# First norm of each layer by token tile: turns, router and shared expert of tile 0 while tile 1 is normalised, and the output product by column halves

## The reference, cut to what matters

```python
for l in range(2):
    h = merged @ w_out[l]                       # 256 x 1024 times 1024 x 1024
    x = layer_norm(DN_ALPHA * x + h, ln1_g[l], ln1_b[l])
    idx, wts = route(x, router_w[l], router_bias[l])       # 1024 -> 64 scores per token, top 8 of 64
    u = x @ shared_w_gate_up[l]                            # 1024 -> 512
    shared = (silu(u[:, :256]) * u[:, 256:]) @ shared_w_down[l]
    y = shared + routed_experts(x, idx, wts, expert_w_gate_up[l], expert_w_down[l])
    x = layer_norm(DN_ALPHA * x + y, ln2_g[l], ln2_b[l])
```

## Time and profile before

| | |
|---|---|
| median of 3 runs | 1595.6 us (1593.86 to 1598.8) |
| profiled execution, its own time | 1594.94 us |
| its span, first to last instruction | 1593.1 us |
| PE busy | 1535.1 us, 96% of the span |
| DVE, ACT busy | 567.2 us, 413.2 us |
| mean granted TensorE clock | 0.983 |
| transfers | 495.85 MB, 311 GB/s over the span |

### The profile page before, as it was taken

How to read it: one execution, slowest core, us unless ns; L and a number is a source line. 1 busy time by engine, 2 the same in 40 slices (tenths; PEclk the granted TensorE clock), 3 DMA queues, 4 the chain that set the end, 5 groups by cost and what they waited for, 6 DMA issues and landing times.

```text
span 1593.1 us, 21647 instructions
## 1 busy us (share of the span) xinstructions
PE 1535.1 (96%) x8770; PEld 954.1 (60%) x8770; DVE 567.2 (36%) x1011; ACT 413.2 (26%) x653; POOL 34.5 (2%) x30
## 2 busy tenths in 40 slices
PE   7999998999999999999789999989999999999996
PEld 7899985554454444445388999865444544544442
DVE  4567735222222222222445677352222222222224
ACT  4545422121111112112235544221211211111111
POOL 0101000000000000000001110000000000000000
PEclk9999998999999999999989999989999999999998
DMA  8544458699999999699733544577999999996991
GB/s 290 174 170 142 155 210 355 250 425 423 418 418 415 405 415 414 248 414 417 279 104 109 186 159 159 213 315 280 428 423 416 420 408 410 417 412 247 415 416 77
DMA packets 79740, 495.85 MB, mean 311 GB/s; under 512 B 6080, under 2 KB 11456, under 8 KB 46656
## 3 DMA queue, kind: packets, MB, share of 16 engines
q1 hardware_dynamic: 77392, 491.31, 76.4%
q10 hardware_dynamic: 2288, 3.67, 0.7%
HBM read 493.92 MB, written 1.05 MB: 311 GB/s over the span
## 4 chain that ended last, share of the span: by engine, by line
PE 93%; DVE 2%; DMA 2%; ACT 1%; issue 1%; SPq 0%; DVEq 0%
PE bank L1384 27%; PE bank L1227 19%; PE bank L1410 14%; PE bank L1339 8%; PE bank L1356 8%; PE bank L1297 4%; PE bank L1184 3%; PE bank L1314 2%; DMA ring_w<-in_w_in 2%; PE bank L1396 1%; PE bank L1371 1%; PE bank L1305 1%; PE bank L1347 1%; ACT w_hi L590 1%; PE bank L1239 1%; PE bank L1265 1%
## 5 line engine op out<-in xcount | busy, mean ns | idle before, releaser
L1227 PE MATMUL bank<-x_hi,w_hi 128*128 128x256 f32 x688 | 198.4, 288 | 3.5 <-ACT arena L639 1.9
L1227 PE MATMUL bank<-x_hi,w_lo 128*128 128x256 f32 x688 | 195.3, 284 | 0.0
L1227 PE MATMUL bank<-x_lo,w_hi 128*128 128x256 f32 x688 | 195.3, 284 | 0.0
L1121 DVE SCALAR_TENSOR_TENSOR hid<-hid,gate_s,bank 128x256 f32<-128x256 f32 x64 | 30.8, 481 | 401.2 <-ACT hid L701 401.2
L1384 PE MATMUL bank<-gu_a,arena 128*64 128x512 f32 x768 | 170.1, 595 | 0.0
L1384 PE MATMUL bank<-arena 128*64 128x512 f32 x768 | 170.1, 595 | 0.0
L1135 DVE TENSOR_TENSOR y_lo<-bank,y_hi 128x512 fp32r<-128x512 f32 x128 | 88.6, 692 | 225.7 <-ACT y_hi L707 225.7
L771 DVE TENSOR_TENSOR w_lo<-ring_w,w_hi 128x2048 fp32r<-128x2048 f32 x63 | 143.9, 2288 | 66.2 <-ACT w_hi L590 66.1
L707 ACT CAST y_hi<-bank 128x512 fp32r<-128x512 f32 x128 | 75.0, 586 | 247.8 <-PE bank L1410 247.8
L1339 PE MATMUL bank<-onehot,xg_hi 128*128 128x256 f32 x512 | 138.8, 304 | 0.0
L1227 PEld LDWEIGHTS bank<-x_hi,w_hi 128*128 128x128 f32 x688 | 132.7, 193 | 7.5 <-issue 4.0
(11 more groups left out here) (186 smaller groups left out, 2010.9 us busy)
## 6 DMA issues: line engine op xcount, KB each, us to landing
gu_a<-in_expert_w_gate_up SPq DMA_DIRECT2D x24, 4096.0 KB, 13.5
arena<-in_expert_w_gate_up SPq DMA_DIRECT2D x24, 4096.0 KB, 14.5
ring_w<-in_expert_w_gate_up SPq DMA_DIRECT2D x32, 2048.0 KB, 10.7
ring_w<-in_w_in SPq DMA_DIRECT2D x25, 2048.0 KB, 8.7
dn_a<-in_expert_w_down SPq DMA_DIRECT2D x24, 2048.0 KB, 11.4
arena<-in_expert_w_down SPq DMA_DIRECT2D x24, 2048.0 KB, 11.3
dn_c<-in_expert_w_down SPq DMA_DIRECT2D x16, 2048.0 KB, 11.5
ring_w<-in_w_out SPq DMA_DIRECT2D x4, 2048.0 KB, 8.8
```

Of the source, the lines that this page charges most:

```text
L1227: ins = mm(b[:, S * c:S * c + S], lhs, rhs, start=(k == 0 and a + w == 0), stop=(k == KD - 1 and a == 1))
```

## The change

The output product runs by column halves: both tiles of half 0, then both tiles of half 1. The SP queue loads the shared expert's first matrix as soon as half 0 is done, and its place in the queue moves ahead of the first transfer of pair 1 (`load_up(l, 1, 1)`).

The tasks `("shared", 0, 0)` and `("shared", 1, 0)` leave the plan. PE now turns tile 0, runs the router of tile 0 and the gate half of the shared product of tile 0, turns tile 1, runs the other half of tile 0, then the router of tile 1, both halves of tile 1, and the rank task last. The shared product writes two banks of the output product, `acc[0][0]` and `acc[0][1]`, instead of task banks, in matmuls of 128 columns. ACT empties turns 0, 1 and 2, takes the square root for tile 1 after turn 1, and makes `xg_hi` of a tile one turn later. DVE makes `sh_t` between `route` and `ranks`.

```diff
@@ plan @@
-    return tasks + [("xt", 1, g) for g in range(4)] + [("router", 0, 0), ("shared", 0, 0), ("rank", 0, 0),
-                                                       ("shared", 1, 0)]
+    return tasks + [("xt", 1, g) for g in range(4)] + [("router", 0, 0), ("rank", 0, 0)]
...
+        bank_shared = acc[0]
@@ SP @@
                     elif BLOCKS[before][0] == "shared_up":
-                        wait_task(sp, bl, ("shared", 1, 0))
+                        sp.wait_ge(shared_up_done, 2 * (bl + 1))
                     elif BLOCKS[before][0] == "out":
-                        sp.wait_ge(h_ready, 2 * TT * (bl + 1))
+                        sp.wait_ge(h_ready, 2 * TT * bl + TT * (BLOCKS[before][1] + 1))
...
+                load_block(l, NB - 2)
                 sp.wait_ge(merged_ready, 4 * (l + 1))
                 load_up(l, 1, 1)
                 sp.wait_ge(h_ready, 2 * TT * (l + 1))
-                for n in range(NB - 2, NB):
-                    load_block(l, n)
+                load_block(l, NB - 1)
                 load_down(l, 1, 1)
 
-                wait_task(sp, l, ("shared", 1, 0))
+                sp.wait_ge(shared_up_done, 2 * (l + 1))
                 load_up(l, 2, 2, (0, 1))
@@ ACT @@
-                    elif kind == "xt" and j % 2 == 0:
+                    elif kind == "xt" and j < 3:
                         wait_task(act, l, task)
                         free(nc.scalar.copy(x_tile(x_t, j), b[:].rearrange("p (c n) -> p c n", c=4)), l, task)
-                        nc.scalar.copy(xg_hi[:, j // 2], ...)
+                        if j == 1:
+                            norm_std(act, l, 0, 1)
+                        if j:
+                            nc.scalar.copy(xg_hi[:, j - 1], ...)
...
-                    elif kind == "shared" and i == 0:
-                        wait_task(act, l, task)
-                        free(nc.scalar.activation(sh_silu, b[:].rearrange("p (c n) -> p c n", c=2), ACT.Silu), l, task)
+                        act.wait_ge(shared_up_done, 2 * l + 1)
+                        nc.scalar.activation(sh_silu, bank_shared[0][:].rearrange("p (c n) -> p c n", c=2),
+                                             ACT.Silu).then_inc(sh_silu_ready, 1)
...
                     if task == ("branch", 2, 3):
-                        for t in range(TT):
-                            norm_std(act, l, 0, t)
+                        norm_std(act, l, 0, 0)
@@ DVE @@
-                            dve.wait_ge(h_ready, 2 * TT * l + 2 * t + h + 1)
+                            dve.wait_ge(h_ready, 2 * TT * l + TT * h + t + 1)
...
-                    elif kind == "xt" and j % 2 == 1:
+                    elif kind == "xt" and j == 3:
...
                     if task == ("router", 0, 0):
                         route(l)
+                        dve.wait_ge(shared_up_done, 2 * (l + 1))
+                        dve.wait_ge(sh_silu_ready, l + 1)
+                        v.tensor_tensor(sh_t, sh_silu, bank_shared[1][:].rearrange("p (c n) -> p c n", c=2),
+                                        ALU.mult).then_inc(sh_ready, 1)
                     if task == ("rank", 0, 0):
                         ranks(l)
                         slots(0)
@@ PE @@
+            def route_tile(l, t):
+                for g in (2 * t, 2 * t + 1):
+                    wait_evac(pe, l, ("xt", 1, g))
+                for k in range(KD):
+                    ins = mm(bank(l, ("router", 0, 0))[:, NE * t:NE * t + NE], x_t[:, k, P * t:P * t + P],
+                             router_sb[:, k, :], start=(k == 0), stop=(k == KD - 1))
+                return ins
+
+            def shared_up(half, t):
+                weights = slot_of_block(BLOCK_OF["shared_up", 0], KD)
+                tokens = slice(P * t, P * t + P)
+                for c in range(2):
+                    col = FE * half + P * c
+                    for k in range(KD):
+                        ins = mm(bank_shared[half][:, S * c + P * t:S * c + P * t + P], weights[:, k, col:col + P],
+                                 x_t[:, k, tokens], start=(k == 0), stop=(k == KD - 1))
+                return ins
...
-                        for t in range(TT):
-                            for h in range(2):
+                        for h in range(2):
+                            for t in range(TT):
...
                     elif kind == "router":
+                        ins = route_tile(l, 1)
...
                     ins.then_inc(bank_ready, 1)
+                    if task == ("xt", 1, 1):
+                        acquire(l, ("router", 0, 0))
+                        route_tile(l, 0)
+                        block_ready(l, BLOCK_OF["shared_up", 0])
+                        shared_up(0, 0)
+                    elif task == ("xt", 1, 3):
+                        shared_up(1, 0)
+                    elif kind == "router":
+                        for half in range(2):
+                            shared_up(half, 1).then_inc(shared_up_done, 1)
...
                     if q == 0:
-                        wait_evac(pe, l, ("shared", 1, 0))
+                        pe.wait_ge(sh_ready, l + 1)
```

More of the change, by code:

```diff
@@ L320, in build @@
         gates_ready = sem("gates_ready")
+        shared_up_done = sem("shared_up_done")
+        sh_silu_ready = sem("sh_silu_ready")
+        sh_ready = sem("sh_ready")
         shared_down = sem("shared_down")
@@ L605, in _ @@
                                 split_high(0, u)
-                    elif kind == "xt" and j % 2 == 0:
+                    elif kind == "xt" and j < 3:
                         wait_task(act, l, task)
                         free(nc.scalar.copy(x_tile(x_t, j), b[:].rearrange("p (c n) -> p c n", c=4)), l, task)
-                        nc.scalar.copy(xg_hi[:, j // 2],
-                                       x_tok[:, j // 2, :].rearrange("p (q k) -> p k q", k=KD)).then_inc(xg_hi_ready, 1)
+                        if j == 1:
+                            norm_std(act, l, 0, 1)
+                        if j:
+                            nc.scalar.copy(xg_hi[:, j - 1],
+                                           x_tok[:, j - 1, :].rearrange("p (q k) -> p k q", k=KD)).then_inc(xg_hi_ready, 1)
                     elif kind == "z":
@@ L963, in _ @@
                             setup()
-                    elif kind == "xt" and j % 2 == 1:
+                    elif kind == "xt" and j == 3:
                         wait_task(dve, l, task)
                         free(v.tensor_copy(x_tile(x_t, j), b[:].rearrange("p (c n) -> p c n", c=4)), l, task)
-                        if j == 3:
-                            for t in range(TT):
-                                dve.wait_ge(xg_hi_ready, TT * l + t + 1)
-                                v.tensor_tensor(xg_lo[:, t], x_tok[:, t, :].rearrange("p (q k) -> p k q", k=KD),
-                                                xg_hi[:, t].bitcast(F32), ALU.subtract).then_inc(xg_lo_ready, 1)
+                        for t in range(TT):
+                            dve.wait_ge(xg_hi_ready, TT * l + t + 1)
+                            v.tensor_tensor(xg_lo[:, t], x_tok[:, t, :].rearrange("p (q k) -> p k q", k=KD),
+                                            xg_hi[:, t].bitcast(F32), ALU.subtract).then_inc(xg_lo_ready, 1)
                     elif kind == "scores":
@@ L1070, in _ @@
                                 ins.then_inc(merged_ready, 1)
[L1071 to L1074, removed]
                     if task in (("pool", 1, 0), ("z", 21, 0)):
```

## The result

| | median us (range) | against before on the same chip, ratio [95% interval] |
|---|---|---|
| before | 1596.3 (1593.86 to 1598.8), 4 runs | |
| after | 1582.92 (1581.64 to 1584.38), 4 runs | 0.9918 [0.9904, 0.9932] |
| after, measured again | 1581.77 (1581.41 to 1584.33), 5 runs | 0.9917 [0.9903, 0.9930] |

The change makes the kernel 13.1 to 13.4 us faster, 0.8%. The profiled execution of after took 1581.64 us, its span is 1579.8 us, 13.3 less than before, and the mean granted clock went from 0.983 to 0.989.

A forecast was written before the change was run, and what follows sets the result against it. PE was taken to bound the kernel, with 93% of the chain of waits. Gains of 7.35 and 7.0 us, together 14.4, less 5.1 for clock falls, gave 9.3 us less: 1586 us, range 1580 to 1592.

The forecast's parts named there:

- some 12 are clock: Both layers, product's end to gather: of 14.4 us gained, some 12 from the clock (router 3.5, turns 1.1, shared half 1.7 a layer).
- turns and their emptying: Tile 0, behind the output product: turns 0.89 us at full clock, then 1.0 us for ACT's emptying, no longer hidden.
- router: Each tile's router: 16 records at full clock, 1.77 us a tile, 3.53 as upper bound.
- shared: Shared product: 128 records of 128 columns at 0.111 us, 14.2 us; upper bound 27.9 us.
- rank and DVE behind it: Before the first gather: rank 0.14 us, then PE idle 2.2 us for DVE's sh_t and ranks, bounds 1.5 and 2.9.
- DVE's choice in time for the rank: Choice released 6.6 us after the router, against 7.1 us of PE work: 0.5 us slack, else a wait up to 0.7.
- pair 1's matrix later at no cost: Pair 1's first matrix queued at 245.5 instead of 232.84 us and not read before 300: costs nothing.
- the gain carried through the experts: Experts' stage: a weight stream that starts earlier keeps its distance, so the gain is carried to the end.
- Load of the shared matrix: Tile 0's gate half: transfer moves from 258.91 to 245.1 us, needed about 262.5; over 17 us to its use, before 14.3.
- Clock falls: Falls before the gather in each layer, 3.4 us in all, and one behind the product, 1.7 us: together 5.1 us lost.
- Rival 1: The clock never falls in the new gaps, so all 14.4 us remain: 1581 us, chance 0.14.
- Rivals 2 to 4: Experts wait for weights, 1595 (0.08); clock stays low over 128-column matmuls, 1617 (0.04); weight loads, 0.218 us a record, 1609 (0.04).

The follow-up runs named there:

- e5: The kernel before with 4 idle matmuls (result unused) put into PE's wait for the norm, no useful work moved: 1583.14 us, 0.9930 of before.
- e8: The changed kernel with the shared matrix loaded as before the change, behind the whole output product and pair 1's first matrix: 1597.30 us, 1.0021 of before.
- e4: The changed kernel with the rank task ahead of tile 1's last shared quarter, another quarter moved behind tile 1's router, sh_t behind the slots: 1576.13 us, 0.9891.
- e2: The changed kernel with 4 idle matmuls behind the rank task, in the idle time before the first gather: 1583.47 us, 0.9945 of before.
- e1: The kernel before with 8 idle matmuls between the turns of tile 0 and those of tile 1: 1590.14 us, 0.9968 of before.
- e3: The changed kernel with sh_t made behind the slots on DVE instead of ahead of the ranks: 1580.87 us, 0.9924 of before.

## Why the prediction was right, and where it was off

- *What bounds, and that the clock is the larger part:* right. Of the 14.4 us, "some 12 are clock"; fillers alone brought 11.3 (e5).
- *Terms on PE:* turns and their emptying 1.7 us (1.9 predicted), router 1.97 and 1.73 (1.77 each), shared 14.4 (14.2), turns 0.88 (0.89), rank and DVE behind it 2.2 (2.3). Sum 22.9 (22.9), and 22.8 in layer 1: gains of 7.4 and 7.1 against 7.35 and 7.0.
- *DVE's choice in time for the rank, the extra copies hidden, pair 1's matrix later at no cost, the gain carried through the experts:* right; the experts of layer 1 to the end took 500.8 us in both profiles.
- *Load of the shared matrix:* right that its slack is enough, and e8 shows what the term hides: with the old order of the queue the change would have been worth less than nothing. The prediction priced the early load at nothing and should have priced its absence.
- *Clock falls, the term that was mis-sized:* "I count a fall in each layer [before the gather], and one fall for the two layers" behind the product, 5.1 us. Behind the product none occurred in any profile of the changed kernel. Ahead of the gather five of eight gaps were followed by one, at 1.8 us each, and filling that gap brought 1.4 us in the medians, not 3.4, a difference that is itself within the noise. With 1.4 in place of 5.1 the sum is 13.0; with five falls in eight gaps, 2.2 us for the two layers, it is 12.2; 13.1 to 13.4 were measured. The nearest row was read as a rule and was one draw: behind 2.52 us of idling the clock fell in before, behind 2.51 (e4) and 2.93 (e2) at the same place it did not, and behind 2.0 it does either.
- *Rival 1 (never a fall, 1581):* nearer than the forecast's 1586, but not what happened: the clock fell in each profile of the changed kernel. The Trainium skill, "TensorE: Matmul & The Clock Gate", section "HAM oscillation — how this bites in real kernels", warns only of idle gaps longer than these of 2 us; the traces here disagree, with falls behind 2.04 us (after) and during e1's router, where no pause was over 0.86.
- *Rivals 2 to 4:* out. Experts as long as before; the clock came back during 128-column records (e8); 0.113 us a record and not 0.218, with PE and its weight loads both busy for 4.00 of 4 us (stretch 261 to 265 of after), so the twice as many loads ran beside the matmuls.

## What to carry to other kernels

When PE waits for a norm, read the granted clock of what follows before pricing the wait: here 3.7 us of idling cost 5.8 and 5.5 us more behind it in the two layers, and fillers alone got that back (e5). When work is moved earlier, move its transfer first, and look at what the last piece of the old order was hiding: a dependent task (here the ranks) goes ahead of the last independent work, not behind it. Read more than one profile before a clock fall is priced as certain: a pause of 1.4 us left the clock up in every profile here, as did the two of 1.51 and 1.60 us in e3, while those of 1.94 to 2.93 us did either.

## What was not expected of the hardware

- The same idle time of 1.94 to 2.04 us brought the clock down in five gaps out of eight; in three of the four executions it did so in one layer and not in the other. At another place 2.93 us left it up (e2).
- The clock fell without a pause over 0.86 us, in a run of turns and 64-column float32 matmuls (e1, layer 0), and stayed up over the same instructions in layer 1.
- A float32 record of 64 columns took 0.11 us at 2.4 GHz (1.73 us for 16) and one of 128 columns 0.113 (7.21 for 64): with 128 x 128 float32 weights, 64 columns were no faster than 128. One of 256 columns took 0.218, so splitting 256 in two costs next to nothing (14.41 us against 13.98).
